# A hybrid decoder trunk: state-space sums and latent attention's compressed rows turned by VectorE and the sync queue instead of TensorE

## The reference

```python
h = _rmsnorm(x, ln_g[l])
u = h @ w_in[l]                       # 6232 columns: gates and the inputs of four mixers
y_a = _gla(...) * silu(g_a)           # gated linear attention
y_b = _ssd_mixer(...)                 # state space: y = scan + xs * D; y * silu(g_b); rmsnorm in 2 groups
y_c = _mla(...) * silu(g_c)           # latent attention
y_d = _dilated_attention(...) * silu(g_d)
x = x + concatenate([y_a, y_b, y_c, y_d]) @ w_out[l]
```

## Time and profile before

| | |
|---|---|
| median of three runs | 824.35 us (823.65 to 824.37) |
| the profiled execution | 823.59 us, span 821.6 us, clock of TensorE 1.00 |
| TensorE matmuls busy | 816.4 us, 99% of the span |
| TensorE weight loads busy (beside the matmuls) | 693.0 us, 84% |
| VectorE busy | 625.2 us, 76% |
| ScalarE busy | 478.2 us, 58% |
| GpSimd busy | 54.1 us, 7% |
| read from HBM | 148 MB, 183 GB/s over the span |

### The profile page before, as it was taken

One profiled execution on the slowest core, in us unless ns is written; L12 is line 12 of the kernel. 1 busy time (PEld: TensorE's weight loads), 2 busy tenths in 40 slices (PEclk: granted clock), 3 DMA queues, 4 the chain that ended last, 5 costly groups with the idle time before them and its releaser, 6 DMA issues.

```text
span 821.6 us, 11397 instructions
## 1 busy us (share of the span) xinstructions
PE 816.4 (99%) x4244; PEld 693.0 (84%) x4244; DVE 625.2 (76%) x1118; ACT 478.2 (58%) x788; POOL 54.1 (7%) x64
## 2 busy tenths in 40 slices
PE   9999999999999999999999999999999999999998
PEld 5888888999888888888888888889998888888886
DVE  6678799876886986678965977979769868965542
ACT  6665534777865566433556464357697665654341
POOL 7200000200200000000000000002012000000000
PEclk9999999999999999999999999999999999999999
DMA  9956634566654445655576655457657433456653
GB/s 333 352 204 211 192 129 153 145 208 180 208 176 154 129 132 201 191 191 187 177 253 184 200 161 169 129 147 200 191 173 220 164 129 129 158 177 210 196 189 119
DMA packets 47607, 150.98 MB, mean 184 GB/s; under 512 B 5504, under 2 KB 6192, under 8 KB 47552
## 3 DMA queue, kind: packets, MB, share of 16 engines
q1 hardware_dynamic: 47040, 149.98, 57.0%
q10 hardware_dynamic: 320, 0.21, 0.1%
q0 software_dynamic: 192, 0.07, 0.1%
HBM read 148.13 MB, written 2.11 MB: 183 GB/s over the span
## 4 chain that ended last, share of the span: by engine, by line
PE 91%; DVE 7%; issue 2%; DMA 1%; SPq 0%; ACT 0%; DVEq 0%
PE gemm L665 26%; PE gemm L674 26%; PE gemm L666 26%; DVE arena L1323 3%; DVE w_lo L1354 2%; PE pairs L857 1%; PE pairs L846 1%; PE pairs L833 1%; PE pairs L838 1%; PE pairs L834 1%; PE pairs L795 1%; PE pairs L731 1%; DVE arena L1433 1%; PE pairs L872 1%; DMA u<-in_xT_dram 1%
## 5 line engine op out<-in xcount | busy, mean ns | idle before, releaser
L1354 DVE TENSOR_TENSOR w_lo<-raw,w_hi 128x1024 fp32r<-128x1024 f32 (+2 forms) x295 | 324.7, 1110 | 144.4 <-ACT w_hi L997 142.9
L665 PE MATMUL gemm<-w_hi,a_hi 128*128 128x512 f32 (+1 forms) x1144 | 421.6, 374 | 0.0
L666 PE MATMUL gemm<-w_hi,a_lo 128*128 128x512 f32 (+1 forms) x1144 | 414.4, 368 | 0.0
L997 ACT ACTIVATE w_hi<-raw 128x1024 fp32r<-128x1024 f32 (+2 forms) x295 | 281.0, 967 | 191.4 <-PE gemm L674 136.1
L674 PE MATMUL gemm<-w_lo,a_hi 128*128 128x512 f32 (+1 forms) x1144 | 281.8, 368 | 0.3
L665 PEld LDWEIGHTS gemm<-w_hi,a_hi 128*128 128x128 f32 x1144 | 215.2, 188 | 35.6 <-issue 1.3
L666 PEld LDWEIGHTS gemm<-w_hi,a_lo 128*128 128x128 f32 x1144 | 215.3, 188 | 33.0
L674 PEld LDWEIGHTS gemm<-w_lo,a_hi 128*128 128x128 f32 x1144 | 203.2, 188 | 36.6 <-DVE w_lo L1354 2.0
L573 POOL TENSOR_TENSOR st<-st,powers 128x4 f32<-128x4 f32 (+2 forms) x8 | 8.6, 1074 | 431.5 <-ACT arena L1075 213.4
L1195 ACT ACTIVATE arena<-arena,st 128x128 f32<-128x128 f32 (+1 forms) x32 | 13.1, 444 | 35.4 <-DVE st L1616 35.4
L1027 ACT ACTIVATE u<-gemm,st 128x512 f32<-128x512 f32 (+1 forms) x40 | 22.1, 605 | 18.8 <-PE gemm L674 18.8
(11 more groups left out here) (200 smaller groups left out, 639.0 us busy)
## 6 DMA issues: line engine op xcount, KB each, us to landing
raw<-in_weights_dram SPq DMA_DIRECT2D x225, 512.0 KB, 4.1
raw<-in_weights_dram SPq DMA_DIRECT2D x64, 278.0 KB, 3.1
raw<-in_weights_dram SPq DMA_DIRECT2D x6, 384.0 KB, 3.4
x<-in_x_dram SPq DMA_DIRECT2D x4, 512.0 KB, 6.2
o<-ssd_rows SPq DMA_DIRECT2D x8, 256.0 KB, 4.9
param_rows<-in_params_dram SPq DMA_DIRECT2D x2, 904.0 KB, 7.1
u<-in_xT_dram SPq DMA_DIRECT2D x3, 512.0 KB, 8.1
out_dram<-x SPq DMA_DIRECT2D x3, 512.0 KB, 6.4
```

The source lines that it names most:

```text
L665: pe.matmul(acc_t[t], a_hi[:, k, tok[t]], hi, start=k == 0, stop=False)
L666: pe.matmul(acc_t[t], a_lo[:, k, tok[t]], hi, start=False, stop=False)
L997: A_(w_hi[:, g % SPLIT, 0:c], raw[:, g % RAW, 0:c], ACT.Copy).then_inc(hi_done, 1)
L1354: TT(w_lo[:, g % SPLIT, 0:c], raw[:, g % RAW, 0:c], w_hi[:, g % SPLIT, 0:c].bitcast(F32), ALU.subtract).then_inc(split_done, 1)
```

## The change

The sixteen transposes a layer of `mla cT` and `ssd yb` leave TensorE, with the two PSUM banks that they took and ScalarE's copy `ssd y`. In their place each tile is turned in two steps. VectorE transposes squares of 32x32 within each quarter of 32 partitions into a new buffer `fold` (128x1024): `mla c squares` at 62 (two instructions of 512 elements in each partition) and `ssd y squares` at 80 (four of 256). Then the sync queue moves the squares across the quarters, 16 transfers each of 32 partitions by 256 columns (1 KB a partition), into `c_squares` and `y_squares` (in the arena); it does so at its places 67 and 85, behind the load of that unit's weights. ScalarE's cT copy now waits for these transfers instead of TensorE and reads SBUF, and stands behind the skip product instead of ahead of it; VectorE's cT_lo reads SBUF too. The gate product waits for the second group of transfers, reads y_squares and writes o in a permuted order, and moves from 93 to 91, ahead of the first maximum. `fold` is used by both, so `ssd y squares` waits for the first group's transfers, and in layer 1 `mla c squares` for the second group's of layer 0.

```diff
+C_SQUARES, Y_SQUARES = 62, 80
...
-          "ssd xs": 62, "mla cT": 64, "mla q 0": Q_AT, "mla q 1": Q_AT, "mla kv 0": KV_AT,
-          "mla kv 1": KV_AT, "ssd Y": 76, "ssd yb": 81, "mla qT": 85, "mla kT": 86, "mla rT": 87, "mla S 0": 89, "mla PT 0": 92,
+          "ssd xs": 62, "mla q 0": Q_AT, "mla q 1": Q_AT, "mla kv 0": KV_AT,
+          "mla kv 1": KV_AT, "ssd Y": 76, "mla qT": 85, "mla kT": 86, "mla rT": 87, "mla S 0": 89, "mla PT 0": 92,
...
+        fold = sb("fold", [P, S * 4])
+        c_squares, y_squares = A(3072, 1024), A(4096, 1024)
+
+        def by_f(row):
+            return row.rearrange("p (k f b) -> p f k b", f=4, b=32)
...
         @block.sync
         def _(sp):
+            def across(to, source, arrived):
+                for i in range(4):
+                    for f in range(4):
+                        sp.dma_start(to[32 * f:32 * f + 32, i * S:(i + 1) * S], source[32 * i:32 * i + 32, f * S:(f + 1) * S]).then_inc(arrived, 16)
...
+                    if n == C_SQUARES + 5:
+                        sp.wait_ge(*reached("dve", l)("mla c squares"))
+                        across(c_squares, fold, c_squares_in)
+                    if n == Y_SQUARES + 5:
+                        sp.wait_ge(*reached("dve", l)("ssd y squares"))
+                        across(y_squares, fold, y_squares_in)
...
-                def ssd_yb():
-                    pe.wait_ge(*dve("ssd yT"))
-                    ps = bank()
-                    for f in range(SSD_DI // P):
-                        for t in range(T):
-                            last = pe.transpose(ps[:, t, f * P:(f + 1) * P], ssd_yT(f)[:, t * P:(t + 1) * P], ident)
-                    last.then_inc(*signal("pe", "ssd yb"))
-                def mla_cT():
-                    pe.wait_ge(*dve("mla cn"))
-                    ps = bank()
-                    for kk in range(4):
-                        for t in range(T):
-                            c = COL["cq"] + kk * P
-                            last = pe.transpose(ps[:, kk // 2, (kk % 2) * S + t * P:(kk % 2) * S + (t + 1) * P], u[:, t, c:c + P], ident)
-                    last.then_inc(*signal("pe", "mla cT"))
...
                 def ssd_xD():
                     act_.wait_ge(*me("ssd silu 0"))
-                    act_.wait_ge(*pe("mla cT"))
+                    act_.wait_ge(*dve("mla c squares"))
-                def ssd_y():
-                    act_.wait_ge(*pe("ssd yb"))
-                    A_(o[:, GB], pair_of("ssd yb"), ACT.Copy).then_inc(*signal("act", "ssd y"))
                 def mla_cT():
-                    act_.wait_ge(*pe("mla cT"))
-                    act_.wait_ge(*me("mla crs sum"))
-                    A_(cT_hi[:, :, :], pair_of("mla cT").rearrange("p b (k s) -> p (b k) s", k=2), ACT.Copy).then_inc(*signal("act", "mla cT"))
+                    act_.wait_ge(c_squares_in, 16 * 16 * (l + 1))
+                    A_(cT_hi.rearrange("p k (t i a) -> p i (k t) a", t=T, i=4), c_squares.rearrange("p (i c a) -> p i c a", i=4, a=32), ACT.Copy).then_inc(*signal("act", "mla cT"))
-                    if n == slot("mla cT"):
-                        mla_cT()
-                        ssd_xD()
+                    if n == 67:
+                        ssd_xD()
+                        mla_cT()
...
+            def turn_squares(to, rows):
+                to = to.rearrange("p (f k t a) -> p t k f a", f=4, k=4, t=T)
+                for t in range(T):
+                    last = v.transpose(to[:, t], rows[:, t].rearrange("p k (f b) -> p k f b", f=4))
+                return last
...
+                    if g == GB:
+                        v.wait_ge(y_squares_in, 16 * 16 * (l + 1))
+                        TT(by_f(o[:, GB].rearrange("p t c -> p (t c)")), y_squares.rearrange("p (f c b) -> p f c b", f=4, b=32),
+                           by_f(gate.rearrange("p t c -> p (t c)")), ALU.mult).then_inc(*sig(f"gated {g}"))
+                        return
...
+                def ssd_y_squares():
+                    v.wait_ge(*me("ssd yT"))
+                    v.wait_ge(c_squares_in, 16 * 16 * (l + 1))
+                    to = fold.rearrange("p (i t k b) -> p k t i b", i=4, t=T, k=4)
+                    for f in range(SSD_DI // P):
+                        last = v.transpose(to[:, f], ssd_yT(f).rearrange("p (t i a) -> p t i a", t=T, i=4))
+                    last.then_inc(*sig("ssd y squares"))
+                def mla_c_squares():
+                    v.wait_ge(*me("mla cn"))
+                    if l:
+                        v.wait_ge(y_squares_in, 16 * 16 * l)
+                    turn_squares(fold, u[:, :, COL["cq"]:COL["cq"] + WB].rearrange("p t (k c) -> p t k c", k=4)).then_inc(*sig("mla c squares"))
...
-                    if n == 93:
+                    if n == 91:
                         gated(GB)
```

More of the change, by code:

```diff
@@ L198 @@
                "ssd xs": ("dve", "ssd xdt"),
-               "ssd cum": ("dve", "ssd row"), "ssd gcol": ("act", "ssd gcol"), "ssd CB": ("dve", "ssd CB"), "ssd Y": ("dve", "ssd yT"), "ssd yb": ("act", "ssd y"),
-               "mla cT": ("dve", "mla cT"), "mla qT": ("act", "mla qT"), "mla kT": ("act", "mla kT"), "mla rT": ("act", "mla rT"),
+               "ssd cum": ("dve", "ssd row"), "ssd gcol": ("act", "ssd gcol"), "ssd CB": ("dve", "ssd CB"), "ssd Y": ("dve", "ssd yT"),
+               "mla qT": ("act", "mla qT"), "mla kT": ("act", "mla kT"), "mla rT": ("act", "mla rT"),
                "dil qT": ("act", "dil qT"), "dil kT": ("act", "dil kT")}
@@ L230 @@
         "gla level 6, gla level 7, gla out, ssd cum, ssd gcol, ssd CB, ssd xs, "
-        "mla cT, ssd Y, ssd yb, mla qT, mla kT, mla rT, "
+        "ssd Y, mla qT, mla kT, mla rT, "
         "mla S 0, mla PT 0, mla S 1, mla O 0, dil qT, mla PT 1, dil kT, mla O 1, dil S 0, dil PT 0, dil S 1, dil O 0, "
@@ L237 @@
         "ssd eA, ssd ln, conv 3 1, gla rs sum, conv 3 0, evac 5, ssd silu 1, "
-        "mla crs sum, ssd gcol, evac 6, ssd silu 0, ssd exp 0, evac 7, mla cT, ssd xD, ssd exp 1, mla q 0, mla q 1, mla rs 0 sum, "
-        "evac 8, mla kv 0, mla kv 1, mla rs 1 sum, dil rs 0 sum, evac 9, dil rs 1 sum, ssd y, mla qT, mla kT, evac 10, "
+        "mla crs sum, ssd gcol, evac 6, ssd silu 0, ssd exp 0, evac 7, ssd xD, mla cT, ssd exp 1, mla q 0, mla q 1, mla rs 0 sum, "
+        "evac 8, mla kv 0, mla kv 1, mla rs 1 sum, dil rs 0 sum, evac 9, dil rs 1 sum, mla qT, mla kT, evac 10, "
         "mla rT, mla P 0, ssd rs sum, mla PT 0, mla P 1, evac 11, dil qT, mla PT 1, dil kT, dil P 0, dil PT 0, "
@@ L246 @@
         "ssd la, conv 1 0, conv 1 1, gla o, conv 1 2, conv 1 3, conv 1 4, conv 1 5, ssd row, conv 0 0, conv 0 1, conv 0 2, "
-        "conv 0 3, conv 0 4, conv 0 5, ssd CB, mla cn, ssd E 0, ssd xdt, mla cT, ssd E 1, ssd M 0, ssd M 1, "
-        "mla n 0 0, mla n 0 1, ssd yT, mla n 1 0, mla n 1 1, mla rope products, mla rope, dil n 0 0, dil n 0 1, "
-        "dil n 1 0, dil n 1 1, dil rope 0 products, dil rope 0, dil rope 1 products, dil rope 1, mla max 0, "
[1 row of a table removed]
+        "conv 0 3, conv 0 4, conv 0 5, ssd CB, mla cn, mla c squares, ssd E 0, ssd xdt, mla cT, ssd E 1, ssd M 0, ssd M 1, "
+        "mla n 0 0, mla n 0 1, ssd yT, ssd y squares, mla n 1 0, mla n 1 1, mla rope products, mla rope, dil n 0 0, dil n 0 1, "
+        "dil n 1 0, dil n 1 1, dil rope 0 products, dil rope 0, dil rope 1 products, dil rope 1, gated 1, mla max 0, "
[1 row of a table added]
         "dil nmax 0, dil P 0, y turn 0, dil max 1, dil nmax 1, dil P 1, dil ri 0, dil O 0, y 2, yT 0, dil ri 1, dil O 1, yT 1, "
@@ L428, in build @@
         warm = sem("warm")
+        c_squares_in, y_squares_in = sem("c_squares_in"), sem("y_squares_in")
         setup_chain = sem("setup_chain")
@@ L899, in _ @@
                 run = {"gla lr": gla_lr, "gla z": gla_z,
-                       "gla out": gla_out, "ssd xs": ssd_xs, "ssd cum": ssd_cum, "ssd gcol": ssd_gcol, "ssd CB": ssd_CB, "ssd Y": ssd_Y, "ssd yb": ssd_yb, "mla cT": mla_cT,
+                       "gla out": gla_out, "ssd xs": ssd_xs, "ssd cum": ssd_cum, "ssd gcol": ssd_gcol, "ssd CB": ssd_CB, "ssd Y": ssd_Y,
                        "mla qT": mla_qT, "mla kT": mla_kT, "mla rT": mla_rT}
@@ L1364, in gated @@
                     v.wait_ge(*act(f"evac {b}"))
-                    v.wait_ge(*(act("ssd y") if g == GB else me({GA: "gla o", GC: "mla O 1", GD: "dil O 1"}[g])))
-                    TT(o[:, g], o[:, g], gate, ALU.mult).then_inc(*sig(f"gated {g}" if g == GB else f"y {g}"))
+                    if g == GB:
[3 more added lines that the diff above has]
+                        return
+                    v.wait_ge(*me({GA: "gla o", GC: "mla O 1", GD: "dil O 1"}[g]))
+                    TT(o[:, g], o[:, g], gate, ALU.mult).then_inc(*sig(f"y {g}"))
                 def y_turn(j, i):
@@ L1602, in smax @@
                     v.wait_ge(*pe(f"{m} S {i}"))
+                    if (m, i) == ("mla", 0):
+                        v.wait_ge(*me(f"gated {GB}"))
                     if i:
```

(4 more changed lines are left out.)

5 lines of the change are left out of this document (2 added, 3 removed), and 2 rows, old and new, of the table ORDER.

## The result

| | before | after |
|---|---|---|
| median of four runs each | 824.17 us (823.65 to 824.37) | 835.02 us (833.68 to 835.43) |
| profiled execution, span | 823.59 us, 821.6 us | 835.01 us, 833.2 us |
| TensorE matmuls busy | 816.4 us, 99% | 817.8 us, 98% |
| TensorE's granted clock, mean | 1.00 | 0.994 |

The ratio of after to before is 1.0129, with an interval from 1.0116 to 1.0142. The forecast was 821.2 us with a range to 826.5; the changed kernel lies 8.5 us above the range.

The account below looks back on a forecast made before the run. TensorE was taken to bound the kernel, its matmuls busy 816.4 of 821.6 us. Removing 3.56 us and adding 2 x 0.2 us of waits gave -3.2 us: from the median 824.35 to 821.2 us, range 820.3 to 826.5.

Parts of the forecast that it names:

- Removed from TensorE: Two groups of eight transposes in each of two layers leave TensorE: 1.78 us a layer, 3.56 us in all.
- Squares on VectorE: VectorE's 32x32 transposes: 0.44 us each for state-space rows (1.75 us), 0.70 for compressed rows (1.4 us).
- The copies from SBUF in runs of 32: cT copies reading SBUF keep their price: 1.03 us on ScalarE, 1.23 on VectorE, give or take 0.1.
- Added to the sync queue: Sixteen small transfers at each place, 0.37 us an issue (0.28 to 0.47), hold the queue 5.9 us (4.5 to 7.5).
- rival 2: Gain eaten: issues of 0.43 to 0.47 us, unit 68 waits 1.65 us a layer, 824.1 us; chance 0.21.
- Landing of a square: A small transfer needs about 2.0 us, at most 4.9; the compressed rows' last square lands at 181.85.
- Rival 3: ScalarE waits at the cT copy for the last square, holding up unit 68: 826.6 to 829.3 us; chance 0.15.
- TensorE's wait: Before unit 68, TensorE waits 0.2 us a layer for that unit's high part.
- Second place: State-space rows, units 80 to 93: costed at 0, margin 2.7 us, or 1.1 at 0.46 us an issue.

Follow-up runs that it names:

- e10_moved: Changed kernel with the compressed rows' 16 transfers on GpSimd, cT copies and projections moved later, state-space transfers in fours behind loads 85 to 88; 820.35 us, ratio 0.9956.
- e6_shapes: Kernel before plus a probe at unit 100 of layer 0: six groups of sync-queue transfers differing in source memory, partitions and bytes; 839.2 us, one run.
- e5_c_gpsimd: Changed kernel with the compressed rows' 16 transfers issued by GpSimd instead of the sync queue; 829.9 us, ratio 1.0074.
- e4_unread: Changed kernel with all 16 transfers issued, but the cT copies read fold and wait for no transfer (rows in wrong order); 834.24 us, ratio 1.0126.
- e1_y_only: Changed kernel with only the state-space rows changed; the compressed rows' transposes are back on TensorE; 822.81 us, ratio 0.9988.
- e7: Only the state-space rows changed, their transfers in fours behind loads 85 to 88 instead of sixteen behind 85; 821.84 us, ratio 0.9974.
- e8_half_spread: Changed kernel with eight compressed-row transfers on the sync queue, eight on GpSimd, and state-space transfers in fours behind loads 85 to 88; 820.87 us, ratio 0.996.
- e9_twelve: Changed kernel with twelve of the compressed rows' transfers on the sync queue and four on GpSimd; 829.43 us, ratio 1.0067.

## Why the prediction was wrong

The forecast was faster by 3.2 us; the kernel is slower by 10.85. Step by step:

- **Removed from TensorE, 3.56 us: right.** In after the last thirds of units 64 and 65 are 1.55 us apart (179.01 to 180.56), where the earlier trace rows has 2.42, and e10_moved gains 3.60.
- **Squares on VectorE: right.** By the groups of after (total us, mean ns of one), 0.41 us each for the state-space rows (forecast 0.44) and 0.69 for the compressed rows (0.70):

```profile
L1571 DVE STREAM_TRANSPOSE fold<-u 128x256 f32<-128x256 f32 x8 | 2.8, 409 | 0.0
...
L1330 DVE STREAM_TRANSPOSE fold<-u 128x512 f32<-128x512 f32 x4 | 2.6, 688 | 0.0
```

  The four quarters of partitions are worked together; the row of one quarter gives the price of all.
- **The copies from SBUF in runs of 32: right.** 1.06 us on ScalarE against 1.03 from PSUM, 1.23 on VectorE as in the earlier trace rows.
- **Added to the sync queue: this step failed.** It put an issue at 0.37 us with bounds of 0.28 to 0.47, and it is 0.63 from start to start. Each row has one end in DRAM (the last one has its source in SBUF and its end in DRAM); the dear issues are those with both ends in SBUF (e6_shapes), and before has none. I had reasoned from the number of partitions, which plays no part (0.59 us with 16 and 32, 0.60 with 128), and took the step after a lone load where all rows that follow another closely say 0.43 or more; by rival 2 that alone was worth the difference between a gain and none. With 0.63 the same working is near the trace: the load of unit 68 goes out at 174.3 + 16 x 0.63 = 184.4, lands 3.1 us later at 187.5, its high part is ready at 188.15, and the wait is 188.15 - 183.75 = 4.4 us (measured 4.65 and 5.17). The bounds were too narrow for a kind of issue that the trace did not have, and narrower than some rows it did have: in the first microseconds of before, between other loads, issues took 0.65 and 0.71 us, which I had left out.

```profile
4.00 0.65 SPq L495 DMA_DIRECT2D raw<-in_weights_dram  x1
...
5.39 0.71 SPq L495 DMA_DIRECT2D raw<-in_weights_dram  x1
```

  The Trainium skill (DMA: Bandwidth & Descriptors, Anatomy of one DMA) puts the dispatch at some 50 ns, for the GpSimd path. Taken as the price of an issue that is twelve times too low for this queue, and ten times for GpSimd's own 0.50 us in e5_c_gpsimd.
- **Landing of a square, 2.0 us: right** (1.9), and so was the judgement that ScalarE's order does not decide with the sync queue as issuer (e4_unread). Rival 3 had the right sign for the wrong reason.
- **What comes after a wait: left out.** I priced TensorE's wait as its length. In layer 0 it cost 4.65 us and another 2.85 at the lower clock, in layer 1 5.17 and 1.46: together 4.3 us that no step of the sum had, nor any rival. Why the clock stays low for longer behind the shorter of the two waits, these runs do not show.
- **Second place at 0: not quite.** Some 0.6 us in after and 1.3 in e1_y_only, both in layer 0 by the starts of the same matmuls, and 1.0 us by the medians of e1 and e7; the margin was right in kind, and used up by the same wrong price.
- **Rivals.** Rival 2 was the mechanism: issues dearer than taken, unit 68's weights behind them. Its price was 0.46 us, so it stopped at 824.1, no change. With 0.63 its waits alone would have given 824.35 - 3.56 + 2 x 4.4 = 829.6; the last 5 us are the clock and waits 0.2 to 0.8 us longer than that.

The rule of the Trainium skill that sends a 128x128 transpose to TensorE (VectorE: DVE Perf Modes, Rules for kernel authors) would here have given the right sign. The runs do not bear it out as a rule for this kernel: the same turning in two steps gains 3.6 us as soon as its issues stand ahead of nothing (e10_moved).

## What to carry to other kernels

An in-order queue that loads weights is a resource with a price per issue, and the lead of the engine it feeds, in microseconds at that place, is all it can spend: here 5.7 us (unit 68 due at 183.75, less 0.65 for its high part, 3.1 for the landing, and 174.3), nine issues, where sixteen were put; eight already cost 0.6 us in layer 1, where one of them took 1.14 us (e8_half_spread). Price an issue by a row with the same memory at both ends, and where there is none, give the unknown a wide upper end and spread the issues, or put them on an idle queue and move the reader back by the longer landing. A wait on TensorE of some microseconds should be counted with a second loss behind it at the lower clock: here 0.3 and 0.6 of the wait's length in after, 0.7 in e5_c_gpsimd and in layer 1 of e9_twelve, and nothing in layer 0 of e9_twelve. And a loss is found by setting the starts of the same matmuls side by side; the idle time that the profile marks was 0.5 us of 1.3 in e1_y_only.

## What the runs showed of the hardware

- An issue on the sync queue takes 0.59 to 0.60 us (median) from SBUF to SBUF, whatever the partitions (16 to 128) and bytes (512 B or 1 KB each), and 0.42 to 0.43 from DRAM to SBUF (e6_shapes); from SBUF to DRAM it is 0.43 (the five stores of before). Single issues take much longer: 1.39 us in layer 1 of after.
- GpSimd issues the same transfers in 0.50 us each, but ScalarE could start on the data only 3.2 us after the last issue had ended in e5_c_gpsimd (183.05 to 186.30) and 2.5 us in e10_moved (182.44 to 184.94), against 1.3 us with the sync queue (184.69 to 186.00, in after).
- After waits of 4.65 to 5.2 us TensorE was granted 1.2 GHz for part of what followed (0.52 over 6.5 us, 0.76 over 6.6); after waits of 2.8 to 2.9 us it was too (0.72 over 6.1 us in layer 0 of e5_c_gpsimd), and after waits of 2.3 us once (0.76 over 6 us, e9_twelve, layer 1) and once not (1.00, layer 0).
